# A two-layer hybrid decoder: sums of down-weight blocks by accumulating DMAs, a new order of the products, and VectorE's split ahead of its evictions

## What is computed

```python
    h2 = rms_norm(x, ln_mlp_pre)
    ff = jnp.square(jax.nn.relu(h2 @ w_up)) @ w_down      # 1024 -> 4096 -> 1024
    return x + rms_norm(ff, ln_mlp_post)
```

## Time and profile before

| | |
|---|---|
| time, median of 3 runs | 1913.14 us (1912.83 to 1913.59) |
| the profiled execution's own time | 1912.04 us |
| its span, first to last instruction | 1910.1 us |
| TensorE (PE) busy, share of the span | 1851.4 us, 97% |
| VectorE (DVE) busy | 1322.6 us, 69% |
| ScalarE (ACT) busy | 754.2 us, 39% |
| GpSimd (POOL) busy | 205.4 us, 11% |
| mean granted TensorE clock | 0.995 |

### The profile page before, as it was taken

One profiled execution on the slowest core, in us unless ns is written; L12 is line 12 of the kernel. 1 busy time (PEld: TensorE's weight loads), 2 busy tenths in 40 slices (PEclk: granted clock), 3 DMA queues, 4 the chain that ended last, 5 costly groups with the idle time before them and its releaser, 6 DMA issues.

```text
span 1910.1 us, 23505 instructions
## 1 busy us (share of the span) xinstructions
PE 1851.4 (97%) x8622; PEld 1489.4 (78%) x8622; DVE 1322.6 (69%) x2128; ACT 754.2 (39%) x1259; POOL 205.4 (11%) x317
## 2 busy tenths in 40 slices
PE   8999999999999999999799999999999999999996
PEld 6877767888888787878578767678888887878784
DVE  6865889753475768586868658887434768585768
ACT  3163352421335544435431533524122355445353
POOL 2221111011220000000012211111112100000000
PEclk9999999999999999999999999999999999999998
DMA  6432213322521231414222322232225222314031
GB/s 243 138 117 82 68 65 97 83 67 78 220 100 53 104 113 64 152 58 144 81 87 94 133 71 68 67 97 72 78 78 220 89 75 81 136 51 165 34 111 44
DMA packets 73218, 190.01 MB, mean 99 GB/s; under 512 B 18384, under 2 KB 30864, under 8 KB 72080
## 3 DMA queue, kind: packets, MB, share of 16 engines
q1 hardware_dynamic: 43200, 159.31, 24.2%
q10 hardware_dynamic: 29904, 29.19, 4.6%
HBM read 177.42 MB, written 11.06 MB: 99 GB/s over the span
## 4 chain that ended last, share of the span: by engine, by line
PE 87%; DVE 6%; issue 4%; ACT 3%; DMA 0%; DVEq 0%; ACTq 0%; SPq 0%
PE psD L1167 22%; PE psD L1169 22%; PE psD L1168 22%; PE psM L1167 3%; PE psM L1169 3%; PE psM L1168 3%; PE psM L1226 2%; DVE d_lo L2459 1%; PE psM L1240 1%; PE psM L1435 1%; PE psM L1233 1%; PE psM L1453 1%; PE psM L1332 1%; PE psM L1441 1%; DVE wide L2469 1%
## 5 line engine op out<-in xcount | busy, mean ns | idle before, releaser
L1167 PE MATMUL psD<-a_hi,w_hi 128*128 128x512 f32 (+2 forms) x1488 | 594.7, 400 | 0.9 <-DVE w_lo L1054 0.6
L1169 PE MATMUL psD<-a_hi,w_lo 128*128 128x512 f32 (+2 forms) x1488 | 575.9, 387 | 0.0
L1168 PE MATMUL psD<-a_lo,w_hi 128*128 128x512 f32 (+2 forms) x1488 | 574.8, 386 | 0.0
L1054 DVE TENSOR_TENSOR w_lo<-raw,w_hi 128x1024 fp32r<-128x1024 f32 x216 | 264.4, 1225 | 134.0 <-POOL w_hi L1153 96.5
L1167 PEld LDWEIGHTS psD<-a_hi,w_hi 128*128 128x128 f32 (+1 forms) x1488 | 279.3, 188 | 75.6 <-issue 21.3
L1169 PEld LDWEIGHTS psD<-a_hi,w_lo 128*128 128x128 f32 (+1 forms) x1488 | 279.0, 187 | 57.8
L1168 PEld LDWEIGHTS psD<-a_lo,w_hi 128*128 128x128 f32 (+1 forms) x1488 | 279.6, 188 | 56.9 <-issue 4.3
L1152 POOL TENSOR_TENSOR w_hi<-raw,tabs 128x1 fp32r<-128x1 f32 x152 | 35.0, 230 | 1278.2 <-PE psD L1169 1247.1
L1153 POOL TENSOR_SCALAR w_hi<-raw 128x1023 fp32r<-128x1023 f32 x152 | 169.4, 1115 | 0.0
L2459 DVE TENSOR_TENSOR d_lo<-d_raw,d_hi 128x1024 fp32r<-128x1024 f32 x104 | 125.9, 1222 | 60.0 <-ACT d_hi L1984 60.0
L1984 ACT CAST d_hi<-d_raw 128x1024 fp32r<-128x1024 f32 x104 | 108.0, 1047 | 128.9 <-DVE d_raw L2436 82.9
(11 more groups left out here) (285 smaller groups left out, 2918.4 us busy)
## 6 DMA issues: line engine op xcount, KB each, us to landing
raw<-in_ws SPq DMA_DIRECT2D x216, 512.0 KB, 3.4
d_raw<-in_wd SPq DMA_DIRECT2D x64, 512.0 KB, 4.5
s_raw<-in_wo ACTq DMA_DIRECT2D x14, 512.0 KB, 11.4
tabs<-in_tab SPq DMA_DIRECT2D x2, 2944.0 KB, 12.3
x<-rows_d ACTq DMA_DIRECT2D x4, 1024.0 KB, 5.8
x<-out ACTq DMA_DIRECT2D x2, 2048.0 KB, 8.2
x<-in_x SPq DMA_DIRECT2D x4, 512.0 KB, 5.9
out<-x SPq DMA_DIRECT2D x4, 512.0 KB, 8.2
```

The source lines that it names most:

```text
L1054: dve.tensor_tensor(w_lo[:, s, :], raw[:, s, :], w_hi[:, s, :].bitcast(F32), ALU.subtract) \
L1167: pe.matmul(out, lhi, rhi, start=start, stop=False, skip_group_check=more)
L1168: pe.matmul(out, lhi, rlo, start=False, stop=False, skip_group_check=more)
L1169: return pe.matmul(out, llo, rhi, start=False, stop=stop, skip_group_check=more)
```

## The change

1. **Weight sums by DMA.** The sums t1 to t4 on VectorE are gone. `d_raw` has nine slots with names (`HOMES`). GpSimd issues nine DMAs a chunk that add a block from HBM onto a slot (`accum_op=ALU.add`), each behind waits for the slot's earlier load or sum and, where the slot was an operand, for its split. Signs are moved so that every weight sum is an addition: the activation sums and the evictions of half 1 subtract in its place (`combine`, `combine2`, `evict`).
2. **Loads.** SyncE loads nine blocks for the first chunk in place of eight; in every chunk b12 again into slots A0 and A1 once P1 has been split (`d_in3`); and for the next chunk the nine slots in the order `FREED`, each behind its wait. These waits stand together after slab 7 of the chunk.
3. **Step order.** P1,0 P5,0 P2,0 P1,1 P2,1 P5,1, then as before. P1 is evicted after step 3, P2 after step 4.
4. **VectorE.** In the down phase `d_rest` comes ahead of the evictions. In the up phase S3 and S1 come first, S2 and S4 (`combine2`) directly behind part A of `f_lo`, ahead of `ahead`.
5. **Rounding.** The next layer's slabs 0 and 1 are rounded by ScalarE (`round_up`), not by GpSimd.

```diff
+HOMES = ("A0", "C0", "B0", "A1", "C1", "E", "B1", "D0", "D1")
+BATCH = {"A0": "d_in0", "C0": "d_in0", "B0": "d_in0", "A1": "d_in1", "C1": "d_in1", "E": "d_in1", "B1": "d_in1", "D0": "d_in2", "D1": "d_in2"}
+FREED = {"B0": ("P2", 0), "B1": ("P2", 1), "C1": ("P5", 1), "D0": ("P3", 0), "D1": ("P3", 1), "A0": ("P7", 0), "A1": ("P7", 1),
+         "C0": ("P4", 0), "E": ("P4", 1)}
+SUMMED = {("P5", 0): ("sum_C0", 1), ("P5", 1): ("sum_C1", 1), ("P6", 0): ("sum_C0", 2), ("P6", 1): ("sum_E", 2),
+          ("P7", 0): ("sum_A", 1), ("P7", 1): ("sum_A", 2), ("P4", 0): ("sum_C0", 3), ("P4", 1): ("sum_E", 3)}
...
+                            for j in range(2):
+                                sp.wait_ge(*on(*split_at(c, "P1", j)))
+                                sp.dma_start(home(f"A{j}"), down_slab(c, "b12", j)).then_inc(*inc("d_in3", 16))
+                            for name, step in FREED.items() if c < CHUNKS - 1 else ():
+                                sp.wait_ge(*on(*split_at(c, *step)))
+                                sp.dma_start(home(name), down_slab(c + 1, *FIRST_IN[name])).then_inc(*inc(BATCH[name], 16))
...
+                    for c in range(CHUNKS):
+                        pool.wait_ge(*on("d_in0", 16 * BATCHES["d_in0"] * (c + 1)))
+                        add(c, "C0", "b11", 0)
+                        pool.wait_ge(*on("d_in1", 16 * BATCHES["d_in1"] * (c + 1)))
+                        add(c, "E", "b12", 1)
+                        add(c, "C1", "b11", 1)
+                        pool.wait_ge(*on("sum_E", 16 * (3 * c + 1)))
+                        add(c, "E", "b22", 1)
+                        pool.wait_ge(*on("sum_C0", 16 * (3 * c + 1)))
+                        pool.wait_ge(*on(*split_at(c, "P5", 0)))
+                        add(c, "C0", "b22", 0)
+                        pool.wait_ge(*on("d_in3", 16 * BATCHES["d_in3"] * (c + 1)))
+                        add(c, "A0", "b22", 0)
+                        pool.wait_ge(*on("sum_A", 16 * (2 * c + 1)))
+                        add(c, "A1", "b22", 1)
+                        pool.wait_ge(*on("sum_C0", 16 * (3 * c + 2)))
+                        pool.wait_ge(*on(*split_at(c, "P6", 0)))
+                        add(c, "C0", "b21", 0)
+                        pool.wait_ge(*on("sum_E", 16 * (3 * c + 2)))
+                        pool.wait_ge(*on(*split_at(c, "P6", 1)))
+                        add(c, "E", "b21", 1)
...
                         for st in range(NSTEP if c < CHUNKS - 1 else WHOLE):
+                            if st and st + RING < NSTEP:
+                                d_rest(c, st + RING)
                             if st in AFTER:
                                 dve.wait_ge(*on("d_done", c * NSTEP + st + 1))
                                 evict_product(c, AFTER[st])
-                            if st and st + RING < NSTEP:
-                                d_rest(c, st + RING)
-                            if st in THEN:
-                                THEN[st][0](c, THEN[st][1])
...
-                    for t, args in ((t3, 1), (t4, 0), (t4, 1)):
-                        t(c, args)
```

More of the change, by code:

```diff
@@ L756, in build @@
             d_lo = sb("d_lo", [P, RING, SLAB], F32R, where=mlp)
-            d_raw = sb("d_raw", [P, len(DOWN_SLOT), SLAB], where=mlp)
+            d_raw = sb("d_raw", [P, len(HOMES), SLAB], where=mlp)
         psD = [ctx.enter_context(nc.psum_tensor(f"psD{i}", [P, S], F32)) for i in range(4)]
@@ L892, in operand, with home, down_slab, landed_at @@
             return d_hi[:, r, :], d_lo[:, r, :]
+        def home(name):
+            return d_raw[:, HOMES.index(name), :]
         def source(st):
[L895 to L901, removed]
+            return home(SOURCE[STEPS[st]])
+        def down_slab(c, b, j):
+            return wd[layer * len(DOWN) + c * CT + DOWN_SLOT[b, j]]
+        def landed_at(c, q, j):
+            if (q, j) in SUMMED:
+                name, n = SUMMED[q, j]
+                return name, 16 * (SUMS[name] * c + n)
+            batch = BATCH[SOURCE[q, j]]
+            return batch, 16 * BATCHES[batch] * (c + 1)
+        def split_at(c, q, j):
+            return "d_lo", c * NSTEP + STEPS.index((q, j)) + 1
         def operand_free(eng, c, st):
@@ L1132, in _ @@
                             sp.wait_ge(*on("d_lo", 0))
-                            sp.wait_ge(*on("T", 0))
                             sp.dma_start(tabs2[:], tab[:, basics:]).then_inc(kept["tables_in"], 16)
[L1135 to L1144, removed]
+                        if m == SL_MLP:
+                            sp.wait_ge(*on("slab_done", SLAB_OF["out0", 0] + 1))
+                        if SL_MLP <= m < SL_MLP + CT:
+                            for name in HOMES[m - SL_MLP:m - SL_MLP + (1 if m < SL_MLP + CT - 1 else 2)]:
+                                sp.dma_start(home(name), down_slab(0, *FIRST_IN[name])).then_inc(*inc(BATCH[name], 16))
+                        if m >= SL_MLP and (m - SL_MLP) % CT == CT - 1:
+                            c = (m - SL_MLP) // CT
+                            for j in range(2):
[4 more added lines that the diff above has]
+                                sp.dma_start(home(name), down_slab(c + 1, *FIRST_IN[name])).then_inc(*inc(BATCH[name], 16))
                 @block.gpsimd
@@ L1158, in _, with add @@
                             round_(layer * NSLAB + m)
[L1159 to L1162, removed]
+                    def add(c, name, b, j):
+                        pool.dma_start(home(name), down_slab(c, b, j), accum_op=ALU.add).then_inc(*inc("sum_" + name[:None if name[0] == "C" else 1], 16))
+                    for c in range(CHUNKS):
[19 more added lines that the diff above has]
+                        add(c, "E", "b21", 1)
                 @block.tensor
@@ L1566, in product @@
                         q, j = STEPS[st]
-                        a, _, bank = PRODUCTS[q]
+                        a, bank = PRODUCTS[q]
                         hi, lo = operand(c, st)
@@ L1961, in round_up @@
                         n = SL_MLP + c * CT + i + 2
-                        if n < NSLAB:
+                        if layer * NSLAB + n < DEPTH * NSLAB:
                             s = (layer * NSLAB + n) % 2
@@ L1978, in d_high @@
                         q, j = STEPS[st]
[L1979 to L1982, removed]
+                        act.wait_ge(*on(*landed_at(c, q, j)))
                         operand_free(act, c, st)
@@ L2418, in _, with combine, combine2 @@
                     lo_x1(READY)
[L2420 to L2448, removed]
+                    def combine(c, p):
+                        dve.wait_ge(*on("f_sq", c * CT + 2 * p + 2))
+                        sig(dve.tensor_tensor(fr[:, S3, :], fr[:, A11, :], fr[:, A21, :], ALU.subtract), "comb")
+                        sig(dve.tensor_tensor(fr[:, S1, :], fr[:, A22, :], fr[:, A21, :], ALU.subtract), "comb")
+                    def combine2(c, p):
+                        dve.wait_ge(*on("comb", 4 * (c * PAIRS + p) + 1))
+                        sig(dve.scalar_tensor_tensor(out=fr[:, S2, :], in0=fr[:, S3, :], scalar=-1.0, in1=fr[:, A22, :],
+                                                     op0=ALU.mult, op1=ALU.subtract), "comb")
+                        dve.wait_ge(*on("comb", 4 * (c * PAIRS + p) + 3))
+                        sig(dve.scalar_tensor_tensor(out=fr[:, S4, :], in0=fr[:, A12, :], scalar=-1.0, in1=fr[:, S2, :],
+                                                     op0=ALU.mult, op1=ALU.subtract), "comb")
                     def f_rest(c, p, part):
@@ L2459, in d_rest, with evict @@
                         sig(dve.tensor_tensor(lo, source(st), f32(hi), ALU.subtract), "d_lo")
-                    def evict(t, half, bank, first=False, minus=False):
+                    def evict(t, half, bank, first=False):
                         w, ps = wide[:, t, half * S:(half + 1) * S], banks[bank][t % 2][:, :]
-                        if first:
+                        if first and half:
+                            sig(dve.tensor_scalar(w, ps, -1.0, None, ALU.mult), "evict")
+                        elif first:
                             sig(dve.tensor_copy(w, ps), "evict")
@@ L2468, in evict @@
                                 own("evict")
-                            sig(dve.tensor_tensor(w, w, ps, ALU.subtract if minus else ALU.add), "evict")
+                            sig(dve.tensor_tensor(w, w, ps, ALU.subtract if half else ALU.add), "evict")
                     def evict_product(c, q):
@@ L2489, in evict_product @@
                             else:
-                                evict(2 + t, 0, "V", minus=True)
+                                evict(2 + t, 0, "V")
                     def gained2(t, half, n):
@@ L2563, in _ @@
                             dve.wait_ge(*on("tile_part", 2 * t + 2))
-                            evict(t, 0, "V", minus=True)
+                            evict(t, 0, "V")
                             total("post_mlp", t, 2 * t + 2)
```

29 lines of the change are left out of this document (13 added, 16 removed).

## The result

The changed kernel takes 1897.74 us (median of 4 runs, 1895.04 to 1899.20), the kernel before in the same comparison 1912.99 (1911.80 to 1913.59). The ratio is 0.9919, 95% interval 0.9902 to 0.9937: 15.2 us faster, where 32 were forecast.

What follows compares the result with a forecast made beforehand. TensorE, busy 97%, bounds the kernel; only its MLP down-phase gaps and VectorE-set ends can go. 20.5 + 7.2 + 5.2 = 32.9 us off 1913.1 gives 1880.2, with half a us added 1881; own range 1876 to 1887.

Steps and rivals of the forecast that it cites:

- The sums by DMA: MLP down phase: GpSimd's adding transfers stay hidden at a landing time of 6.0 us, so they cost nothing.
- landing time L: A DMA sum's time from wait to landing: taken as 6.0 us, bounds 3.4 and 11.4.
- All other sums have five us or more: Down phase: sums other than those worked out for A0, A1 and C0's third have at least five us to spare.
- 12(L - 7.8): Cost in us over six whole chunks if A1's sum comes late for step 11; hidden up to L = 7.8.
- Rival 1: Sums are slow and become the wait, sharing engines with the next chunk's loads: 1913 to 1944 us, chance 0.15.
- Rival 2: Sums a little late, L from 6.3 to 9.5, costing ends and chunks: 1897 us at L = 8.5, chance 0.14.
- the wide range: 1876 to 1908 us, holding the forecast, rivals 3 and 4 and most of 2: chance 0.8.
- The chain up to step 11: Down phase: A1's load lands at 12 us, its sum at 12 + 2L; step 11 wants it by 29.9 less 2.4.
- VectorE off the chain: Whole down phases: with weight sums gone and low parts first, all four delays at steps 3 to 6 go.
- the thin margin of 0.1 us: Down phase: step 4's low part ends at 10.8 us, the step is due at 10.88.
- 20.5 us in whole chunks: Six whole down phases: gaps of 3.57 us each go, less 0.15 a chunk for a thin margin.
- The ends: Last chunks of layers 0 and 1: gains start at 23.0 us, so the ends move by 7.2 and 5.2 us.
- Costed at nothing: Negated copies, sums with a factor, step order, SyncE's waits, GpSimd's availability and added DMA traffic: no cost.

Runs made afterwards that it cites:

- experiment 1: The changed kernel without GpSimd's nine accumulating DMAs a chunk and their waits, loads kept, so some weights lack their sums: 1879.82 us, ratio 0.9828.
- act_round: The kernel before with only the next layer's slabs 0 and 1 rounded by ScalarE: 1911.66 us, ratio 0.9993.
- apart_A: The changed kernel with separate counts for A0 and A1, each sum issued once its block has landed, not in series: 1880.54 us, ratio 0.9832.
- old_order: apart_A with the step order of before (P1,0 P2,0 P1,1 P2,1 P5,0 P5,1) and the waits that belong to it: 1927.18 us, ratio 1.0074.

## Why the prediction was right in part

- **The size: one term failed.** The step that failed is "The sums by DMA", in two places. First the landing time L, taken as 6.0 from a plain load's row and treated as one number. A0's sum took 5.74 and 5.62 in the last chunks, 6.42 and 7.66 in the first chunk of each layer, and 9.44 to 10.11 beside the next chunk's loads in the second and third. The bounds 3.4 and 11.4 held; the choice between them was nearly right for the last chunks and wrong for the others. Second, "All other sums have five us or more": E's third had none. In each of the six whole phases GpSimd issued it just when A1's sum had landed (0.24 us after the cast of step 11 began), so the series is three long. By the prediction's own numbers it lands at 12 + 3L, and step 13 wants it by 35.4 less 2.4, which hides L up to 7.0 only.
- **Where the 17.7 us went.** From the first matmul of each step against its due time, over the six phases: step 11 adds 6.7 us, step 12 3.7, step 13 3.3, and the half clock level behind two of the stands 3.4; 0.6 is left over. The formula 12(L - 7.8) counts step 11 alone and has no clock. L = 9.3 would give 17.7 by it, but that fits a sum with terms missing.
- **The rivals.** Rival 1 had the mechanism. Rival 2 gave 1897 for L = 8.5, and the time came out there, inside the wide range too, but by other parts: 8.8 us of its loss was to be in the ends, where nothing was lost. That is luck.
- **The chain up to step 11 held.** A1's load was to land at 12 us (A0's sum went at 11.4), and in the second and third chunks of both layers TensorE's first long wait is at step 11, as foreseen.
- **VectorE off the chain: right.** Steps 3 and 4 are on time in every whole chunk, steps 5 and 6 within 0.16 us, and the low part of step 3 ends 7.3 to 7.4 us in (7.35 forecast). One reading was off: VectorE's share isn't highest in the whole down phases (86%), but in layer 0's last chunk (43.99 of 50.68 us, 87%). The rows are VectorE's in the phase from 729.61 on; the thin margin of 0.1 us held.

```profile
732.85 0.42 DVE L2468 SCALAR_TENSOR_TENSOR gt<-gt 128x256 f32<-128x256 f32 x1
733.30 0.42 DVE L2471 SCALAR_TENSOR_TENSOR gt<-gt 128x256 f32<-128x256 f32 x1
...
735.79 1.23 DVE L2483 TENSOR_TENSOR d_lo<-d_raw,d_hi 128x1024 fp32r<-128x1024 f32 x1 [2.06 <-ACT d_hi L2024]
```

- **20.5 us in whole chunks: right as the value of all else.** Without the sums it was 20.7 (249.90 - 229.23), and the time 1879.8 where the sum of terms had 1880.2.
- **The ends: right, but for one reason given.** 7.2 and 5.2 were forecast; 50.68 - 43.50 = 7.2 and 58.42 - 53.28 = 5.1 came. The gains start 23.07 and 22.92 us in, as worked out (23.0). GpSimd's slab, however, accounts for only 0.9 of the 2.0 us by which layer 0's gains started later than layer 1's: in `act_round` they start 29.35 us in, in place of 30.27. Ahead of step 4's low part VectorE splits a slab of the next layer (1.14 us), which layer 1 has not; that is about the rest, read from the timeline and not tested. The answer to the earlier trace rows:

```profile
924.46 1.29 DVE L2522 TENSOR_TENSOR wide<-wide,sqs 128x512 f32<-128x512 f32 x2
...
1866.54 1.28 DVE L2522 TENSOR_TENSOR wide<-wide,sqs 128x512 f32<-128x512 f32 x2
```

- **"Costed at nothing": half right.** SyncE's queue cost nothing (experiment 1). The step order matters: without it the sums lose 46.6 us. The rounding by itself can't be told from nothing.
- **The Trainium skill's estimate** of 4.4 us for a sum (from DMA: Bandwidth & Descriptors, "Anatomy of one DMA", and Collectives: The Full Stack, "Why ReduceScatter is half of AllGather") was too low: 5.6 at best. That adding doubles the work is borne out by the packets (10.9% against 5.7% of the engines). The Trainium skill's rule on shared SBUF access (SBUF — State Buffer, "Who interferes with whom") was right for the rounding (0.76 against 1.62). For the issue of transfers, which was open, no effect shows: a combination beside an issue (649.16, issue from 648.59 on) took 0.42 as elsewhere, and the ends are no longer with sums than without.

**Left open.** What holds E's third sum back. The trace names only "issue" (7.44 us at 760.25), and each time it ends as A1's sum lands. It occurs in `apart_A` too (4.49 us before 665.30, 5.83 before 1601.08), where it makes no step late. With copies GpSimd issued three transfers in 1.57 us, and in `old_order` three sums in 2.66, without such a hold. No run tests it by itself, nor what steps 12 and 13 would gain if E's third sum went earlier in the changed kernel.

## What to carry to other kernels

A transfer that takes over an engine's work has to be timed beside what it will really meet: the loads that the same change lets go at that moment, and its predecessor in a series. Count the series first, and every transfer that is issued behind it: with the series broken, sums of 8.8 us in the median cost nothing here. And once work has left an engine, ask again what order suits it: an order that was right while it was full (split first: 3.9 us gained) was wrong once it had room and no sum was waited for (5.95 us lost), and with nothing moved at all, two lines in a better place gave 10.1 us.

## What the hardware showed that was not expected

- A DMA that adds 512 KB onto SBUF took 5.6 to 5.7 us in the last chunks, without a next chunk's loads, a copy by the same queue 3.7 to 3.9. Beside those loads the sum took 9.4 to 10.1 us in the second and third chunks, the copy 4.8 to 7.8. Issuing a sum held GpSimd for 0.86 to 0.89 us, mostly (a copy 0.53), and the packets of sums took 10.9% of the engines' span against 5.7%.
- Two stands of TensorE, of 2.56 and 1.86 us, were each followed by 3.4 us at the half clock level in whole down phases that otherwise ran at the full level. The stands in the other whole phases, 1.33 us at most, were not.
